# Mixer output kept in SBUF, an mLSTM-first merge without a barrier, and attention scores issued ahead of the transposes, in a one-core decoder layer

## The reference

```python
x = x + 0.5 * _swiglu(_rmsnorm(x, ffn1_norm), ...)
z = _rmsnorm(x, mix_norm) @ w_in                       # RWKV-7 | mLSTM | gates g_a, g_b
y_rw = rwkv7(z_rw)       # 8 heads of 64: token shift, LoRA decay, delta-rule scan, group norm, gate
y_ml = mlstm(z_ml)       # 4 heads of 128: conv, exponential gates, chunkwise matrix memory, norm, gate
merged = sigmoid(g_a) * (y_rw @ w_up_rw) + sigmoid(g_b) * (y_ml @ w_up_ml)
x = x + merged @ w_out
x = x + _memory_attention(_rmsnorm(x, xa_norm), _rmsnorm(mem, mem_norm), wq, wkv, wo)
x = x + 0.5 * _swiglu(_rmsnorm(x, ffn2_norm), ...)
out = _rmsnorm(x, final_norm)

def _memory_attention(hq, hm, wq, wkv, wo):            # 4 heads of 256 over 256 memory tokens
    s = einsum(q, k) * 256 ** -0.5
    p = softmax(s)
    return einsum(p, v).reshape(seq, 1024) @ wo
```

## Time and profile before

| | us |
|---|---|
| median of 3 runs | 3053.16 |
| lowest and highest | 3051.81, 3053.58 |
| the profiled execution, its own time | 3048.96 |
| its span, first to last instruction | 3047.2 |
| granted TensorE clock, mean over the span | 0.983 |

### The profile page before, as it was taken

The page is one execution under the profiler, slowest core; times in us unless marked ns, Lnnn a source line. Parts: engine busy times, 40 slices in busy tenths (PEclk is TensorE's granted clock), DMA queues, the critical chain, the costliest instruction groups (busy, mean ns, idle before and its releaser), DMA issues.

```text
span 3047.2 us, 38944 instructions
## 1 busy us (share of the span) xinstructions
PE 2900.0 (95%) x15102; PEld 2427.4 (80%) x15102; DVE 1278.3 (42%) x1206; ACT 580.3 (19%) x897; POOL 1215.0 (40%) x651
## 2 busy tenths in 40 slices
PE   7999999999999999969999986999899999999996
PEld 6888888888888888868788875887788888888885
DVE  5331331334557331056666654541344321331334
ACT  3100000002001221035555531120412100000001
POOL 3333333334444366534444333333033333333332
PEclk9999999999999999989999998999999999999998
DMA  3111111113222233331132105421011111111111
GB/s 131 48 48 48 48 48 49 49 42 124 93 99 97 103 118 118 106 88 41 40 59 57 43 8 176 145 75 49 0 41 42 49 48 49 48 48 48 49 46 71
DMA packets 108715, 205.00 MB, mean 67 GB/s; under 512 B 14672, under 2 KB 64976, under 8 KB 108392
## 3 DMA queue, kind: packets, MB, share of 16 engines
q1 hardware_dynamic: 85136, 141.15, 15.7%
q10 hardware_dynamic: 23512, 62.90, 5.5%
HBM read 165.12 MB, written 38.86 MB: 67 GB/s over the span
## 4 chain that ended last, share of the span: by engine, by line
PE 40%; issue 8%; POOL 3%; DVE 3%; ACT 1%; DMA 1%; DVEq 0%; POOLq 0%; ACTq 0%; SPq 0%
PE G L607 12%; PE G L608 12%; PE G L609 12%; PE G L824 1%; POOL AL L549 1%; PE G L977 1%; DMA ysg<-y_d 1%; PE G L748 0%; ACT sx L1338 0%; DVE px L1822 0%; DVE mx L1814 0%; POOL kap L529 0%; PE G L969 0%; POOL rho L531 0%; DVE xT L1882 0%
## 5 line engine op out<-in xcount | busy, mean ns | idle before, releaser
L568 POOL TENSOR_TENSOR whi<-raw,zero 128x1024 fp32r<-128x1024 f32 (+1 forms) x215 | 402.2, 1871 | 1439.8 <-PE G L609 1429.2
L607 PE MATMUL G<-hhi,whi 128*128 128x512 f32 x2288 | 893.6, 391 | 17.2 <-DVE hlo L1426 17.2
L608 PE MATMUL G<-hlo,whi 128*128 128x512 f32 x2288 | 891.3, 390 | 0.0
L609 PE MATMUL G<-hhi,wlo 128*128 128x512 f32 x2288 | 891.2, 390 | 0.0
L571 POOL TENSOR_TENSOR wlo<-raw,whi 128x1024 fp32r<-128x1024 f32 (+1 forms) x215 | 521.8, 2427 | 16.9
L607 PEld LDWEIGHTS G<-hhi,whi 128*128 128x128 f32 x2288 | 430.1, 188 | 108.4 <-issue 15.2
L609 PEld LDWEIGHTS G<-hhi,wlo 128*128 128x128 f32 x2288 | 430.1, 188 | 89.9
L608 PEld LDWEIGHTS G<-hlo,whi 128*128 128x128 f32 x2288 | 430.2, 188 | 89.4 <-issue 0.7
L607 PE MATMUL G<-ahi,whi 128*128 128x512 f32 x960 | 374.5, 390 | 2.7 <-DVEq L411 2.7
L608 PE MATMUL G<-alo,whi 128*128 128x512 f32 x960 | 374.2, 390 | 0.0
L609 PE MATMUL G<-ahi,wlo 128*128 128x512 f32 x960 | 374.2, 390 | 0.0
(11 more groups left out here) (315 smaller groups left out, 3249.9 us busy)
## 6 DMA issues: line engine op xcount, KB each, us to landing
raw<-in_wg SPq DMA_DIRECT2D x44, 512.0 KB, 3.5
raw<-in_wu SPq DMA_DIRECT2D x44, 512.0 KB, 3.6
raw<-in_wd SPq DMA_DIRECT2D x32, 512.0 KB, 3.5
raw<-in_ml_in SPq DMA_DIRECT2D x16, 512.0 KB, 3.5
zml_d<-po ACTq DMA_DIRECT2D x16, 512.0 KB, 2.6
gates_d<-po ACTq DMA_DIRECT2D x16, 512.0 KB, 2.7
zm<-zml_d SPq DMA_DIRECT2D x8, 1024.0 KB, 5.9
sg<-gates_d ACTq DMA_DIRECT2D x16, 512.0 KB, 5.2
```

Source lines behind the costliest of these rows:

```text
L568: nc.gpsimd.tensor_tensor(hi, raw[:, k, 0:w], zero[:].to_broadcast([P, w]), ALU.add).then_inc(hi_made, 1)
L607: nc.tensor.matmul(dst, wh, hi, start=start, stop=False)
L608: nc.tensor.matmul(dst, wh, lo, start=False, stop=False)
L609: return nc.tensor.matmul(dst, wl, hi, start=False, stop=stop)
```

## The change

Four things, all in the second third of the program.

1. `y_d` is gone. DVE and POOL write the mixer results of each segment straight into an SBUF tile `yres` of 128 x 8 x 1024 (mLSTM in rows 0 to 3, RWKV-7 in rows 4 to 7). All stores to `y_d`, the loads of it, `ysg`, and the waits on them go. The tiles are laid out anew so that `yres` and the merge's `yhi` and `ylo` fit beside what the last segment still needs.
2. The first `up` unit has buffers of its own, `uraw`, `uhi`, `ulo`. SP loads it ahead of the first segment's loads, and POOL splits it at the end of iteration 7. SP loads the other seven from the moment PE's last `gate` is done; POOL splits the second one in iteration 8 ahead of `ysq`, and the third right after the last `y4` (`behind=3`).
3. The barrier between mixers and merge goes. ACT and DVE split the four mLSTM chunks (`yhi` and `ylo` 4 to 7) inside iteration 8: two on ACT before `Un`, two after it; the four RWKV-7 chunks after the last `y4`. PE starts the merge right after the last group-norm product with the mLSTM halves of units 0 and 1, then the RWKV-7 half of unit 0 chunk by chunk, then that of unit 1. Later units take their halves in the old order. ACT loads the first gates in iteration 8.
4. Attention: PE's round i becomes S of segment i for heads 0 to 2, T of i-1, S for head 3, O of i-1. `qs` of the next segment is copied after S of this one (`next_queries`), and the copy to `pxt` is two copies of half the size with a wait each. The last front round is written out.

```diff
         def mixers_io():
...
             sp.wait_ge(rows_out, 4 * 16)
+            sp.dma_start(uraw[:, 0, :], a["up"][0]).then_inc(raw_in[u0 % 2], 16)
             pipelined(sp, iteration)
-            sp.wait_ge(phase_end, 3 * MIX_DONE)
+            sp.wait_ge(*f_pe.at("gate", LAST))
...
+        def split_unit(u, src, hi, lo):
+
+            pool.wait_ge(raw_in[u % 2], (u // 2 + 1) * 16)
+            tt(hi, src, zero[:].to_broadcast([P, KD * P]), ALU.add).then_inc(hi_made, 1)
+            pool.wait_ge(hi_made, u + (credit + 1))
+            tt(lo, src, hi.bitcast(F32), ALU.subtract).then_inc(split_made, 1)
...
+            def half(bank, k, n, ready=None, wh=whi, wl=wlo):
+                part = slice(n * RC, (n + 1) * RC)
+                return product(bank, k, range(n * RC, (n + 1) * RC), yhi[:, part, :], ylo[:, part, :], ready, wh, wl)
+
+            k = (c.unit + 1) % 2
+            assert bank_dve(c.dve) is G[3]
+            dve_bank(c.dve)
+            unit_ready(c.unit)
+            pe.wait_ge(*sp_dve.at("l1", 1))
+            pe.wait_ge(*b_act.at("Un", LAST))
+            half(bank_dve(c.dve), 0, 1, None, uhi, ulo)
+            act_bank(c.act + 1)
+            unit_ready(c.unit + 1)
+            pe.wait_ge(*b_dve.at("dS", LAST))
+            half(bank_act(c.act + 1), k, 1)
+            pe.wait_ge(*b_dve.at("ve", LAST))
+            dve_bank(c.dve + 1)
+            half(bank_dve(c.dve + 1), 0, 0, output_chunk, uhi, ulo).then_inc(unit_used, 1)
+            half(bank_act(c.act), k, 0).then_inc(unit_used, 1)
...
             if back:
-                store_output(j)
+                act.wait_ge(*b_pool.at("y4", j))
             activation(flat(gout[:]), g2[:, 0, :], ACT.Copy).then_inc(*F.sig("gev"))
...
+        def split_output(n):
+            activation(yhi[:, (n + RC) % KD, :], yres[:, n, :], ACT.Copy).then_inc(*sp_act.sig(f"c{n % 2}"))
...
         pipelined(dve, iteration)
-        barrier(dve, c)
-        split_load(yhi, ylo)
         merge()
```

More of the change, by code:

```diff
@@ L479, in _ @@
                 mixers_io()
+                for o in range(1, n):
+                    load((u0 + o) % 2, "up", o, u0 + o)
+                continue
             rounds = 1 if m % 2 == 0 or n == 1 else 2
@@ L508, in iteration @@
             j = i - 1
+            up = next(u for names, n, tiles, first, u in runs() if names == ["up"])
             def output():
@@ L609, in tile3, with product @@
             return nc.tensor.matmul(dst, wl, hi, start=False, stop=stop)
-        def product(bank, k, tiles, hi, lo, chunk_ready=None):
+        def product(bank, k, tiles, hi, lo, chunk_ready=None, wh=whi, wl=wlo):
             if chunk_ready:
@@ L1002, in _ @@
         pipelined(pe, iteration, ahead)
-        barrier(pe, c)
         merge()
@@ L1645, in iteration @@
                 tt(beta[:], kka[:], Pi[:, :, 1:DEC], ALU.mult).then_inc(*F.sig("beta"))
+            if not front:
+                for n in range(RC):
+                    split_output(n)
             if back:
```

195 lines of the change are left out of this document (103 added, 92 removed).

## The result

The changed kernel takes **3002.94 us** in the median of four runs (3000.31 to 3006.61), where the kernel before, beside it on the same chip, takes 3052.48. The ratio is 0.9839, with a 95% interval of 0.9822 to 0.9856, so some 49 us are gone. The profiled execution took 3000.31 us, its span is 2998.5 us against 3047.2, and the granted TensorE clock over the span is 0.989 (0.983 before).

What follows compares the result with a forecast made beforehand. TensorE was taken to be busy nearly throughout, so only its idle and low-clock time could be won. 31.3 + 3.8 + 2.2 - 1.7 + 11.0 = 46.6 us saved, giving 3002.4 profiled, 3007 as median; range 2997 to 3019.

Steps and rivals of the forecast that it cites:

- Rival A: Clock stays at its upper level in all loop rounds (+2.3) and from 1810 on (another 3): 3001 us; chance 14%.
- Handover: From mixers to merge, up to the end of unit 1: 31.3 us saved, bounds 29.6 and 33.9.
- The low stretch from U on: End of the mixers, 8 us from 1810 on at about half speed: forecast left it unchanged, Rival A saved 3 us.
- The collision in iteration 8: Mixers' last iteration, mLSTM `ylo` chunks on VectorE beside GpSimd's early split: costed at nothing, with 5 us of cover left.
- a low stretch behind chunk 0: Merge, after the two-microsecond gap between chunks 0 and 1: 1.7 us lost, the handover's pessimistic bound of 29.6 us saved.
- The collision behind `y4`: Merge start: GpSimd's split of unit 2 and VectorE's RWKV-7 `ylo` hold each other up; handover saves 31.3 us, not 33.9.
- gap of about 2 us: Sign of being right: TensorE gap between chunks 0 and 1 of unit 0, with a `ylo` of over 2 us.
- the forecast's two ends: End of TensorE's handover work, through unit 1: 1849.6 with the split's collision, 1847.0 without it.
- The store: Mixer loop, ScalarE's store gone: `alpha` wait 0.63 us shorter in each of 6 rounds, 3.8 us saved, bounds 0 and 3.8.
- The clock in the loop: Three of six mixer rounds had a low clock; half of that taken, 2.2 us saved, bounds -1.5 and 4.5.
- `uraw` ahead of `zs`: Start of the mixers, `zs` load behind 512 KB: 1.7 us lost, between 0.4 and 2.3.
- Attention: Attention rounds fall from 9.61 to 8.1 us, TensorE-bound: 11.0 us saved, bounds 8 and 12.

Runs made afterwards that it cites:

- rw_first: Changed kernel with the merge's first two units taking the RWKV-7 half ahead of the mLSTM half; 3014.80 us, ratio 0.9880.
- awake: Changed kernel with ten extra unread matmuls on TensorE ahead of its wait for `ysq` in iteration 8; 3002.76 us, ratio 0.9842.
- best2: best1 with extra unread matmuls at more idle places of TensorE, in iteration 0 and in attention; 2995.91 us, ratio 0.9822.
- store_back: Changed kernel with ScalarE's store of the RWKV-7 result put back ahead of the copy to `gout` in iterations 1 to 7; 3010.35 us, ratio 0.9863.
- store_awake: store_back with three extra unread matmuls on TensorE ahead of its wait for `alpha`; 3010.15 us, ratio 0.9864.
- uraw_late: Changed kernel with the load of the first up unit (`uraw`) issued behind the first segment's loads instead of ahead; 2998.18 us, ratio 0.9831.
- third_late: Changed kernel with GpSimd's split of the third up unit held back until VectorE has made the last `ylo`; 3000.41 us, ratio 0.9834.
- best1: Changed kernel with the edits of uraw_late, second_late, third_late and awake together; 2998.25 us, ratio 0.9825.
- second_late: Changed kernel with GpSimd's split of the second up unit behind `ysq` instead of ahead of it; 3000.63 us, ratio 0.9833.
- attn_old: Changed kernel with attention in the old order, one whole copy to `pxt`, and `qs` copied in its own round; 3011.45 us, ratio 0.9877.
- barrier_back: Changed kernel with the barrier of TensorE, ScalarE and VectorE put back between mixers and merge; 3009.33 us, ratio 0.9864.
- four_heads: Changed kernel with all four heads' scores ahead of attention's transposes instead of three; 3009.30 us, ratio 0.9865.

## Why the prediction was right, point by point

The forecast was 3007, the result 3002.94, inside 2997 to 3019. The mechanisms that it priced were all seen. Of the 3.7 us between the sum's 3006.6 and the result, 2.1 are terms (48.7 us gone in the traces, 46.6 forecast), and 1.6 are the step from a profiled execution to a median, taken as 4.2 us and now 2.6. Rival A, at 3001, names the mechanism for the terms, and both its conditions came: all loop rounds, and the stretch from U on, at the upper clock. The second is in part luck: of the eleven traces without the store, eight have 7.73 us from U to the mean product, but rw_first, awake and best2 have 9.3 to 11.6 with the same TensorE code up to there, but for best2's extra matmuls in iteration 0.

**Handover.** 31.3 us forecast, 31.9 measured (1.12 to 0.69 in the wait for `gout`, and 70.68 to 39.22 from U to the end of unit 1). That is right by errors that cancel. The low stretch from U on, which I left as it was, is gone: 3.2 more saved, A's "another 3". The collision in iteration 8, which I costed at nothing, took 1.2 of them back; at the clock that I had assumed it costs nothing, as store_back shows. The low clock at the variance product, for which the forecast had no term (its bound was for a low stretch behind chunk 0), cost 1.0. And even with that product at 1.12 us the way from its start to the end of unit 1 is 26.3 us where I had 25.8.

The 1.0 is the variance product's own length, not the merge's. The RWKV-7 chunks hang on that product: where it takes 1.12 us, chunk 1 is ready 16.2 us behind its start and unit 1 ends after 26.28 (store_back) and 26.27 (store_awake); where it takes 2.08, chunk 1 is ready after 17.2 and unit 1 ends after 27.24. The merge's own low stretch cost nothing: store_back has it and store_awake has not; and uraw_late, whose clock comes back 1.3 us sooner there, ends unit 1 after 27.21. TensorE lost 3.0 us in all (its twelfth merge matmul starts 6.37 us behind the variance product, 3.41 in awake), and for all but the 1.0 it would otherwise have waited for the chunks.

**The collision behind `y4`.** Seen as described, in the very pair of instructions, but the "gap of about 2 us" between chunks 0 and 1 was 1.0, of which 0.81 is idle. TensorE, 3 us late from the low clock, used part of the gap up. Its price, taken away in third_late, was 1.2 us, where the forecast's two ends (1849.6 and 1847.0) make it 2.6. The second end is wrong by the forecast's own pieces: 1836.7 and 10.9 us of halves are 1847.6, so the bound should have been 33.3 us and the collision 2.0. And 1.2 holds for a TensorE that is late itself. At the upper clock, which the forecast assumed, awake needs 26.16 us from the variance product to the end of unit 1, best1 24.51 with 0.8 of its own in the Newton step ahead of the chunks: by these two traces the collision is worth 1.7 us as it stands, and some 2.4 by an estimate that takes the 0.8 off.

**The store.** 0.63 a round forecast, from one round without a store. The rounds measure 0.52 between the two traces (60.74 to 60.22) and 0.6 in the experiment. Right, a little large.

**The clock in the loop.** I took half of the three low stretches, 2.2 us; all three went, 4.6 us. In the eleven traces of this case without the store every one of the 66 loop rounds takes 60.1 to 60.3 us; in the two with the store and nothing else, three mean products each are long. Of the terms with a price that half was the most mis-sized, and the one round in the earlier trace rows with the short wait had told the truth.

**`uraw` ahead of `zs`.** 1.7 forecast, 1.2 between the traces, 1.1 by experiment.

**Attention.** 11.0 forecast, 10.6 and 10.5 measured. Rounds 8.16 for 8.1; the last value product ran at the lower clock (5.44 for 3.84) where before the `wo` product had done so, which comes to the same (19.51 us from that product to the end of the first `wo` unit in both).

**Not on the list.** Iteration 0 takes 63 us in some executions and up to 66.8 in others, whichever kernel: by the traces 63.4 before, 63.2 changed, 66.5 third_late, 66.8 second_late, 66.6 store_back. The start of attention varies too: from the first scores to the first value product the traces of kernels with the new order and three heads ahead take 11.75 us (uraw_late, rw_first) to 16.31 (store_back), the changed kernel 13.44, by how much of the first and second scores runs at the lower clock. So the 10.6 us of attention holds to a few us in any one execution. Both profiled executions that I compared were of the short kind, which may be one reason why both lie below their medians (3048.96 and 3053.16; 3000.31 and 3002.94).

## What to carry to other kernels

A small instruction on a slow engine (0.4 us of DMA issue on ScalarE) can cost twice: its own time at the next wait, and the clock behind it. When work is moved early "into idle time" on GpSimd, look for what VectorE has in its list behind the instructions that it will hold, not only for who reads those. And price a removed stall against what TensorE would have waited for next: of 3.0 us lost to the low clock here the 1.0 in the product on which the chunks hang cost all of itself, and the 2.0 behind it nothing.

## What the runs showed of the hardware

**A low stretch moves.** Between U and the merge's first matmuls every trace but best1 has part of the stretch at the lower clock. Times from U to the mean product, and of the variance product:

| kernels | U to mean product | variance product |
|---|---|---|
| before, store_back, store_awake | 10.93, 10.87, 12.71 | 1.12, 1.12, 1.13 |
| awake | 11.41 | 1.02 |
| changed, uraw_late, third_late, attn_old, barrier_back, four_heads (`ysq` wait 3.12) | 7.73 in all | 2.07 or 2.08 |
| second_late (`ysq` wait 1.90) | 7.73 | 2.08 |
| rw_first | 11.63 | 1.52 |
| best1 | 7.73 | 1.02 |
| best2 | 9.29 | 1.02 |

Where TensorE had come through the first idle places at the upper clock, it fell at the next one, unless that was filled. Having been low once is no cover: rw_first is slow at the variance product again, and store_back at the merge's start. At the end of attention it was the same between the last value product and `wo`. Why rw_first and awake fell early, though their code up to there is that of the changed kernel, is open.

**VectorE and GpSimd hold each other up, but not always.** In the changed kernel's merge, beside GpSimd's `whi` (1842.50 to 1845.27) and `wlo` (1845.35 to 1847.74):

```profile
1844.57 1.22 DVE L1851 TENSOR_TENSOR sg<-sg,G 128x1024 f32<-128x1024 f32 x1
1845.93 2.90 DVE L1854 TENSOR_TENSOR mo<-mo,sg 128x1024 f32<-128x1024 f32 x1
```

The product with an operand in PSUM (G) takes its 1.22 us beside GpSimd's work, the sum of two SBUF tiles takes 2.90 instead of 1.23. It holds the other way round too: that `whi` takes 2.77 us instead of 1.89, and the one VectorE instruction with two SBUF operands beside it is `hlo<-mo,hhi`, which had started 0.21 us ahead of it. The page SBUF — State Buffer of the Trainium skill, section "SBUF: two separate sides", says just this, that VectorE contends when both its inputs are in SBUF, and the rows agree; the Newton step of 1.49 us in best1 is a third form (scalar-tensor-tensor) with the same fate.
